# A fused two-block model on one core: second input's squares in pairs, S5 lag matrices in full, S5 parameter chain in two parts

## The chip, the cores and the metric

One core of one Trainium2 chip. The metric is the device time of one execution in microseconds; the time of a version is the median of its runs.

## What is computed

The reference runs two residual blocks over 1024 tokens of 1024 features, all in float32. Block one: RMS norm, a large input projection, gated linear attention and differential attention side by side, an output projection, then a convolutional gated FFN of width 2816. Block two adds a positional code to the result and applies an "even" mixer and an "odd" mixer. What the change touches is around the even mixer:

```python
xl = x + sincos_2d(n_tok, x.shape[-1])                    # second input
hl = rmsnorm(xl, norm_g[0]) * (1.0 + scale) + shift
# S5: 48 groups of 16 channels, 64 complex states each, both directions
step = exp(log_step); lam_bar = exp(lam * step)
b_bar = ((lam_bar - 1.0) / lam) * b
s = associative_scan(linear_recurrence, (lam_bar, u @ b_bar))
y = s.real @ c_re - s.imag @ c_im      # forward + backward + d * u
```

The kernel evaluates the recurrence in chunks of CT = 8 steps. In a chunk, the output is a product of the chunk's inputs with a block matrix made of per-lag blocks (the lag matrix, 8 x 16 rows for each group), plus a product of the state ahead of the chunk with the matrices called cp.

## The kernel before, in words

The kernel is a chain of stages; each is a block in which the five engines run their own programs and wait on semaphores by count. A projection (`project`, L134) goes strip by strip: SyncE loads a weight strip of 128 x 1024, ScalarE rounds it to a high part, GpSimd makes the low part (L233), TensorE multiplies high by high, high by low and low by high in 128 x 512 tiles (L263), and VectorE or ScalarE evacuates PSUM. Strips 0 and 1 go together. Strip i + 2 waits for its low part and for the evacuation of strip i (in the same PSUM half). The low part of strip i is made on GpSimd in the order of its program.

**Output projection of block one** ("mix", 8 strips). Beside it, `S5Parameters` (L797) computes exp(lam * step), its powers and factors on VectorE in some 80 small dependent operations: `steps` (18) and `angles` (23) ahead of the first evacuation, `first_power` and `raise_powers` behind strip 1's, `factors` behind strip 2's. Every operation waits for the one before it (`then`, L863). `steps` first waits for three loads, issued behind the 4 MB load of x. ScalarE takes two sines behind the high part of strip 2. GpSimd copies the powers (`place_powers`, behind the low part of strip 3, waiting for `raised`) and computes b_bar (`place_inputs`, behind the low part of strip 4), always ahead of the next low part.

**FFN** (`gated_ffn`, L2274). 22 rounds of gate, down and val strips. Beside it, `StepMatrices` builds the S5 matrices for 3 groups in each of 16 rounds: GpSimd forms products, TensorE turns them and forms lag blocks (L2176), VectorE takes these out of PSUM (`take_taps`, L2181) into a tile of 16 partitions, and SyncE stores cp (L2103), then bt (L2108) and the lag tile in one DMA (L2110). `take_taps` waits until the lag tile of the round before is stored, and the next gate strip on TensorE waits for `taken`.

**Entry into block two** (`IntoBlockTwo`, L2533, at the end of the FFN). VectorE scales the eight rows of x; GpSimd adds the code to rows 0 to 3, VectorE to rows 4 to 7 (L2550). For the next RMS norm ScalarE squares each row into one of two buffers (L675) and TensorE adds up each row over the partitions, 8 matmuls with a column of ones on 8 tiles of 128 x 128 (L680). A square waits for the count two rows back. Mean, root and inverse come in the next block (the input projection "u" of the even mixer), in which ScalarE first rounds the context (L2674), GpSimd makes its low part (L2678), and TensorE waits for that ahead of `spread` (L603), which copies the inverse to all partitions.

**Scan and outputs** (`scan_and_outputs`, L2695). VectorE runs the scan over chunks, 159 steps of four small operations. TensorE meanwhile forms the updates, the strips for the z and Fourier parts, and the Fourier transform. Behind the scan come the outputs, 8 batches of 6 groups, over two buffers: TensorE makes, group by group, the lag product (L2919) and two state products (L2921, L2922); VectorE (L3042) and ScalarE (L2989) gather the states, two copies each; ScalarE applies gelu (L2979) and stores. SyncE loads a batch's cp (one DMA) and its lag matrix in eight DMAs, one for each row block of 16 partitions (L2818), once the batch two back is done. So one batch is in work while the next is loaded only if its buffers are free.

```python
def load(b, s, turn, first):
    if not first:
        sp.wait_ge(done, b - 1)
    sp.dma_start(cp[s], ...)
    for j in range(CT):
        a = (CT - 1 - j) * SH
        sp.dma_start(taps[s][j * SH:(j + 1) * SH, :, :], g.dram["taps"][:, bass.ds(b * GB, GB), a:a + P])
```

## Time and profile before

| what | value |
| --- | --- |
| median of 3 runs | 2517.22 us (2515.45 to 2518.70) |
| profiled execution: its time | 2514.42 us |
| profiled execution: span from first to last instruction | 2512.7 us |
| TensorE matmul busy | 2284.7 us (91%) |
| VectorE busy | 1441.7 us (57%) |
| GpSimd, ScalarE busy | 746.1 us (30%), 701.4 us (28%) |
| mean granted TensorE clock | 0.945 |

The page's row of 40 slices shows TensorE at nine tenths or more nearly everywhere in the FFN. The lower digits after the FFN (slice 24, clock digit 6) and around slices 29 and 30 (clock digits 7 and 8) are the entry into block two and the S5 outputs; the dip at slices 9 to 11 is the output projection of block one. In a timeline row the number in brackets is the engine's idle time ahead of the row and what ended it. Where a wait has several conditions the row names the one that came last by the profile; if that was long done, it was another, often a DMA. "x2" merges two instructions, and the start-to-start distance of such rows is the pace.

### The profile page before, as it was taken

The numbers are of one execution on the slowest core, as the hardware profiler recorded it, in microseconds if no ns is written. First come the engines' busy times: TensorE is split into PE (matmuls) and PEld (weight loads), VectorE is DVE, ScalarE is ACT, GpSimd is POOL, SyncE is SP. The second block draws the span as 40 slices with busy tenths as digits, with TensorE's granted clock in tenths as the row PEclk, the third lists the DMA queues.
The fourth block names the chain that finished last, engine by engine and source line by source line (L and its number), as shares of the span: only waits on it lengthen the run. The fifth ranks groups of instructions, "written<-read, shape, count | busy, mean of one in ns | idle before, by whom it ended". The sixth has DMA issues, their size and how long they took to land. (4 is left out here: it accounts for less than half of the span.)

```text
span 2512.7 us, 29091 instructions
## 1 busy us (share of the span) xinstructions
PE 2284.7 (91%) x11596; PEld 1867.8 (74%) x11596; DVE 1441.7 (57%) x2138; ACT 701.4 (28%) x862; POOL 746.1 (30%) x439
## 2 busy tenths in 40 slices
PE   5999987997889999999999989889965898999986
PEld 3887875676667888888888878778845686878875
DVE  4665435894648887677765663329881424731223
ACT  4104412675122222222222223224124322111121
POOL 0212220112517656655662221110000541221240
PEclk8999988999989999999999996899978998999998
DMA  6596421333113333333332111252236322111111
GB/s 244 209 304 183 125 93 52 109 111 134 43 42 97 111 104 105 116 113 113 113 119 73 51 42 67 76 160 83 96 98 197 146 114 70 51 42 51 42 51 67
DMA packets 108303, 264.98 MB, mean 105 GB/s; under 512 B 9415, under 2 KB 52839, under 8 KB 105065
## 3 DMA queue, kind: packets, MB, share of 16 engines
q1 hardware_dynamic: 105172, 258.04, 31.1%
q10 hardware_dynamic: 3000, 5.15, 0.6%
q8 instruction: 89, 1.46, 0.2%
q14 instruction: 42, 0.34, 0.0%
HBM read 222.79 MB, written 57.13 MB: 111 GB/s over the span
## 5 line engine op out<-in xcount | busy, mean ns | idle before, releaser
L2342 POOL TENSOR_TENSOR w_lo<-w_staged,w_hi 128x1024 fp32r<-128x1024 f32 x66 | 162.5, 2462 | 371.6 <-ACT w_hi L2437 371.5
L233 POOL TENSOR_TENSOR w_lo<-w_staged,w_hi 128x1024 fp32r<-128x1024 f32 (+1 forms) x34 | 83.2, 2449 | 254.8 <-ACT w_hi L200 254.7
L1263 PE MATMUL ps_in<-h_hi,w_hi 128*128 128x512 f32 x400 | 126.6, 398 | 9.4 <-DVE h_lo L648 9.1
L1255 POOL TENSOR_TENSOR w_lo<-w_staged,w_hi 128x1024 fp32r<-128x1024 f32 x23 | 58.1, 2527 | 229.1 <-ACT w_hi L1242 229.1
L366 POOL TENSOR_TENSOR w_lo<-w_staged,w_hi 128x1024 fp32r<-128x1024 f32 x24 | 58.0, 2418 | 228.4 <-ACT w_hi L349 228.4
L374 PE MATMUL ps_odd<-o_hi,w_hi 128*128 128x512 f32 x384 | 121.0, 397 | 4.2 <-DVE o_lo L648 4.2
L1263 PE MATMUL ps_in<-h_lo,w_hi 128*128 128x512 f32 x400 | 124.4, 392 | 0.0
L1263 PE MATMUL ps_in<-h_hi,w_lo 128*128 128x512 f32 x400 | 124.0, 391 | 0.0
L2437 ACT CAST w_hi<-w_staged 128x1024 fp32r<-128x1024 f32 x66 | 69.0, 1045 | 188.4 <-PE ps_dn L2378 188.4
L2248 DVE SCALAR_TENSOR_TENSOR ada_acc<-x_ctx,cond,ada_acc 128x512 f32<-128x512 f32 x112 | 119.8, 1100 | 2.0
L374 PE MATMUL ps_odd<-o_lo,w_hi 128*128 128x512 f32 x384 | 118.8, 391 | 0.0
L374 PE MATMUL ps_odd<-o_hi,w_lo 128*128 128x512 f32 x384 | 118.7, 390 | 0.0
L2362 PE MATMUL ps_up<-f_hi,w_hi 128*128 128x512 f32 x352 | 109.9, 394 | 4.6 <-DVE f_lo L648 4.0
L2362 PE MATMUL ps_next<-f_hi,w_hi 128*128 128x512 f32 x352 | 112.1, 400 | 0.0
L2362 PE MATMUL ps_up<-f_hi,w_lo 128*128 128x512 f32 x352 | 109.3, 392 | 0.0
L2362 PE MATMUL ps_up<-f_lo,w_hi 128*128 128x512 f32 x352 | 109.2, 392 | 0.0
L2362 PE MATMUL ps_next<-f_lo,w_hi 128*128 128x512 f32 x352 | 108.6, 390 | 0.0
L2362 PE MATMUL ps_next<-f_hi,w_lo 128*128 128x512 f32 x352 | 108.5, 389 | 0.0
L2487 DVE SCALAR_TENSOR_TENSOR x<-ps_n,mod,x 128x1024 f32<-128x1024 f32 x66 | 84.5, 1280 | 36.8 <-PE ps_n L2378 34.5
L200 ACT CAST w_hi<-w_staged 128x1024 fp32r<-128x1024 f32 (+1 forms) x34 | 34.8, 1024 | 246.4 <-PE ps_u L263 60.7
L1263 PEld LDWEIGHTS ps_in<-h_hi,w_hi 128*128 128x128 f32 x400 | 73.8, 189 | 27.0 <-issue 12.2
L2001 DVE CUSTOM_DVE_ANT_0 att_s<-ps_s,att_bias 128x1024 f32<-128x1024 f32 x64 | 75.8, 1223 | 23.7 <-PE ps_s L1920 14.6
(473 smaller groups left out, 5648.5 us busy)
## 6 DMA issues: line engine op xcount, KB each, us to landing
w_staged<-in_w_ff SPq DMA_DIRECT2D x66, 512.0 KB, 3.6
x_ctx<-in_w_ada SPq DMA_DIRECT2D x48, 512.0 KB, 5.1
x_in<-in_w_ada SPq DMA_DIRECT2D x16, 1024.0 KB, 8.0
scratch_bias<-scratch_line SPq DMA_DIRECT2D x32, 512.0 KB, 7.5
att_bias<-scratch_bias SPq DMA_DIRECT2D x32, 512.0 KB, 3.2
w_staged<-in_w_in SPq DMA_DIRECT2D x17, 512.0 KB, 4.6
ada_w<-in_w_ada SPq DMA_DIRECT2D x8, 1024.0 KB, 19.4
scratch_cp<-ff_shared SPq DMA_DIRECT2D x16, 384.0 KB, 5.8
```

Of the source, the lines that this page charges most:

```text
L200: nc.scalar.copy(st.hi[i % 2][:, 0:widths[i]], st.staged[i % 2][:, 0:widths[i]]).then_inc(st.hi_ready, 1)
L233: nc.gpsimd.tensor_tensor(st.lo[i % 2][:, 0:widths[i]], st.staged[i % 2][:, 0:widths[i]], st.hi[i % 2][:, 0:widths[i]].bitcast(F32), ALU.s ...
L366: nc.gpsimd.tensor_tensor(st.lo[i % 2][:, :], st.staged[i % 2][:, :], st.hi[i % 2][:, :].bitcast(F32), ALU.subtract).then_inc(st.split, 1)
L374: last = nc.tensor.matmul(ps[i % 2][:, a:a + BANK], w[i % 2][:, k * P:(k + 1) * P], r[:, k, a:a + BANK], start=(k == 0 and part == 0), sto ...
L1255: nc.gpsimd.tensor_tensor(st.lo[i % 2][:, :], st.staged[i % 2][:, :], st.hi[i % 2][:, :].bitcast(F32), ALU.subtract).then_inc(st.split, 1)
L1263: last = nc.tensor.matmul(ps[i % 2][:, a:a + BANK], u[i % 2][:, k * P:(k + 1) * P], r[:, k, a:a + BANK], start=(k == 0 and part == 0), sto ...
L2001: nc.vector.tensor_tensor_reduce(e[n % 2][:, i, :], ps_s[:, i, :], bias[n % 2][:, :], 1.0, -3.0e38, ALU.add, ALU.max, top[:, n, i:i + 1]). ...
L2248: v.scalar_tensor_tensor(acc, here, by, acc, ALU.mult, ALU.add).then_inc(self.weighted, 1)
L2342: nc.gpsimd.tensor_tensor(st.lo[i % 2][:, :], st.staged[i % 2][:, :], st.hi[i % 2][:, :].bitcast(F32), ALU.subtract).then_inc(st.split, 1)
L2362: last = nc.tensor.matmul(ps_up[which][:, a:a + BANK], w[i % 2][:, k * P:(k + 1) * P], r[:, k, a:a + BANK], start=(k == 0 and part == 0), ...
L2437: nc.scalar.copy(st.hi[i % 2][:, :], st.staged[i % 2][:, :]).then_inc(st.hi_ready, 1)
L2487: nc.vector.scalar_tensor_tensor(x[:, k, :], ps_dn[k % len(ps_dn)][:, :], gate_f[:, k:k + 1], x[:, k, :], ALU.mult, ALU.add).then_inc(adde ...
```

## The change

Three edits, independent of each other in place.

First, the parameter chain. The load of lam is issued first, with its own semaphore, and `steps` runs on VectorE ahead of the wait for x; `angles` runs behind strip 0's evacuation; the sines go behind the high part of strip 3; `place_inputs` is split in halves, behind the low parts of strips 4 and 5.

Second, the squares. All eight squares have buffers of their own. GpSimd adds two pairs of them (1+0, 2+3), VectorE the others, down to two tiles, and TensorE adds up two tiles over the partitions rather than eight. Mean, root and inverse move into the FFN's block. The wait for the context's low part comes behind `spread`.

Third, the lag matrices. In the FFN each round's lag tile is stored in eight DMAs (three, three and two, over three units of SyncE's program) as the full block matrix, and `take_taps` waits for all eight of the round before. In the outputs a batch is loaded in two DMAs, there are three buffers for it (the third in rows of 1 KB), TensorE makes the lag products of a batch ahead of its state products and those of batches 0 and 1 ahead of the scan's end, VectorE gathers three quarters of the states and ScalarE one, and the Fourier folds come behind the gathers of batches 2 and 3.

```diff
@@ project
             def begin():
+                if beside is not None:
+                    beside.first(sp)
                 for b in before:
                     b.sync(sp)
...
+            if beside is not None:
+                beside.vector(dve, -1)
             for b in before:
                 b.vector(dve)
-            if beside is not None:
-                beside.vector(dve, -1)
@@ S5Parameters
+    def first(self, sp):
+        sp.dma_start(self.lam, self.g.dram["s5_lam"]).then_inc(self.lam_loaded, 16)
...
     def scalar(self, act, i):
-        if i == 2:
+        if i == 3:
             self.sines(act)
     def vector(self, dve, i):
         if i == -1:
             self.steps(dve)
+        if i == 0:
             self.angles(dve)
...
-        if i == 4:
-            self.place_inputs(pool)
+        if i in (4, 5):
+            self.place_inputs(pool, i - 4)
@@ StepMatrices, gated_ffn
-        sp.dma_start(self.g.dram["taps"][:, b * MB:(b + 1) * MB, :], ...).then_inc(self.taps_stored, 16)
+        self.store_lags(sp, b, range(0, 3))
+    def store_lags(self, sp, b, lags):
+        groups = slice((b % 2) * MB, (b % 2 + 1) * MB)
+        for j in lags:
+            sp.dma_start(self.g.dram["toeplitz"][b // 2, j * SH:(j + 1) * SH, groups, :],
+                         self.taps[:, :, CT - 1 - j:2 * CT - 1 - j, :].rearrange(...)).then_inc(self.taps_stored, 16)
...
-            dve.wait_ge(self.taps_stored, 16 * b)
+            dve.wait_ge(self.taps_stored, 16 * CT * b)
...
+                if i >= 9 and i % 3 == 0 and (i - 9) // 3 < mats.N:
+                    mats.store_lags(sp, (i - 9) // 3, range(3, 6))
+                if i >= 10 and i % 3 == 1 and (i - 10) // 3 < mats.N:
+                    mats.store_lags(sp, (i - 10) // 3, range(6, CT))
@@ IntoBlockTwo
+        v, sq = self.nc.vector, self.sq
+        dve.wait_ge(self.squared, 6)
+        v.tensor_tensor(sq[4], sq[4], sq[5], ALU.add).then_inc(self.dve_added, 1)
+        dve.wait_ge(self.pool_added, 2)
+        v.tensor_tensor(sq[1], sq[1], sq[2], ALU.add).then_inc(self.dve_added, 1)
+        dve.wait_ge(self.squared, 8)
+        v.tensor_tensor(sq[6], sq[6], sq[7], ALU.add).then_inc(self.dve_added, 1)
+        dve.wait_ge(self.dve_added, 3)
+        v.tensor_tensor(sq[4], sq[4], sq[6], ALU.add).then_inc(self.dve_added, 1)
+        self.second.mean(dve)
+        self.second.inverse(dve)
...
+        for a, b in ((1, 0), (2, 3)):
+            pool.wait_ge(self.squared, b + 1)
+            pool.wait_ge(self.squared, a + 1)
+            self.nc.gpsimd.tensor_tensor(self.sq[a], self.sq[a], self.sq[b], ALU.add).then_inc(self.pool_added, 1)
...
-        for k in range(KD):
-            self.second.count(pe, k)
+        for half, (ready, sq) in enumerate(((2, self.sq[1]), (4, self.sq[4]))):
+            pe.wait_ge(self.dve_added, ready)
+            for j in range(second.tiles):
+                last = self.nc.tensor.matmul(second.ps[:, j:j + 1], sq[:, j * P:(j + 1) * P], self.g.ones[:, 0:1], ...)
@@ scan_and_outputs
+            load(0)
+            load(1)
+            for s in range(2):
+                sp.wait_ge(z_stored[s], 16 * (KD // 2))
+            sp.wait_ge(by_pe, FNET_IN)
+            load(2)
+            for b in range(ROOMS, N):
+                if b == 5:
+                    for i in range(S):
+                        sp.wait_ge(folded, 3 * (i + 1))
+                        sp.dma_start(g.dram["yf"][i], yf[i]).then_inc(y_stored, 16)
+                sp.wait_ge(done, b - ROOMS + 1)
+                load(b)
...
+            for b in range(2):
+                tap_products(b)
+            for b in range(N):
+                if b >= 2:
+                    tap_products(b)
+                state_products(b)
```

In `tap_products(b)` TensorE waits for the batch's two loads and, from batch 2 on, for the gelu of batch b - 2; in `state_products(b)` for both gathers.

## Rows read from the trace of the kernel before

**Rows 1.** Timeline of VectorE, output projection: start us, us, engine, line, operation, idle before.
```profile
627.84 2.02 DVE L873 TENSOR_SCALAR s_lam<-s_lam 128x48 f32<-128x48 f32 x1 [22.61 <-DMA s_par<-in_s_c]
...
641.54 1.28 DVE L3180 SCALAR_TENSOR_TENSOR x<-ps_mix,mod,x 128x1024 f32<-128x1024 f32 x1
...
654.28 0.36 DVE L927 TENSOR_TENSOR s_pw<-s_pa,s_pb 128x192 f32<-128x192 f32 x1
...
715.73 1.28 DVE L3180 SCALAR_TENSOR_TENSOR x<-ps_mix,mod,x 128x1024 f32<-128x1024 f32 x1 [7.24 <-PE ps_mix L263]
```

**Rows 2.** Timeline of TensorE, same stage; each row is a pair of matmuls.
```profile
642.97 1.19 PE L263 MATMUL ps_mix<-mix_hi,w_hi 128*128 128x512 f32 x2 [5.55 <-DVE x L3180]
...
647.22 0.62 PE L263 MATMUL ps_mix<-mix_hi,w_lo 128*128 128x512 f32 x2
...
666.29 0.61 PE L263 MATMUL ps_mix<-mix_hi,w_lo 128*128 128x512 f32 x2
...
681.23 1.22 PE L263 MATMUL ps_mix<-mix_hi,w_hi 128*128 128x512 f32 x2 [2.79 <-POOL w_lo L233]
```

**Rows 3.** Timeline of GpSimd, same stage.
```profile
611.00 18.80 POOL L731 TENSOR_TENSOR mix_lo<-mixed,mix_hi 128x1024 fp32r<-128x1024 f32 x8 [36.34 <-ACT mix_hi L725]
...
654.71 2.04 POOL L965 COPY s_par<-s_pw 64x432 f32<-64x432 f32 x1 [6.52 <-DVE s_pw L927]
...
664.79 2.42 POOL L233 TENSOR_TENSOR w_lo<-w_staged,w_hi 128x1024 fp32r<-128x1024 f32 x1
...
678.82 5.66 POOL L233 TENSOR_TENSOR w_lo<-w_staged,w_hi 128x1024 fp32r<-128x1024 f32 x2
```

**Rows 4.** Timeline of TensorE, entry into the second block.
```profile
1567.30 3.55 PE L680 MATMUL ps_next<-ones,ff_val 128*128 128x1 f32 x16
...
1577.67 3.78 PE L603 MATMUL ps_next<-consts,rms_cols_n 128*128 128x128 f32 x16 [6.82 <-POOL e_lo L2678]
...
1585.42 1.41 PE L263 MATMUL ps_u<-e_hi,w_hi 128*128 128x512 f32 x3 [3.97 <-DVE e_lo L648]
```

**Rows 5.** Timeline of VectorE, same entry.
```profile
1548.52 4.62 DVE L2550 TENSOR_TENSOR x<-x,consts 128x1024 f32<-128x1024 f32 x4
```

**Rows 6.** Timeline of GpSimd, same entry.
```profile
1540.34 7.48 POOL L2550 TENSOR_TENSOR x<-x,consts 128x1024 f32<-128x1024 f32 x4 [2.12 <-DVE x L2563]
```

**Rows 7.** Timeline of ScalarE, same entry.
```profile
1571.14 1.90 ACT L2674 CAST e_hi<-x_ctx 128x2048 fp32r<-128x2048 f32 x1 [5.97 <-PEq L2302]
```

**Rows 8.** Timeline of TensorE, S5 outputs.
```profile
1877.97 0.77 PE L2919 MATMUL ps_strips<-x,over_lo 128*128 128x128 f32 x2 [16.40 <-ACT over_hi L2989]
...
1882.95 0.39 PE L2919 MATMUL ps_strips<-x,over_lo 128*128 128x128 f32 x2
...
1888.08 0.39 PE L2922 MATMUL ps_strips<-over_hi,over_lo 128*128 128x128 f32 x2
...
1893.55 0.79 PE L2919 MATMUL ps_strips<-x,over_lo 128*128 x2 [5.08 <-ACT over_hi L2989]
```

**Rows 9.** Timeline of ScalarE, S5 outputs.
```profile
1874.99 5.81 ACT L2989 COPY over_hi<-s_hist 64x768 f32<-64x768 f32 x4 [12.37 <-DVE s_hist L3030]
...
1935.70 0.81 ACT L2979 ACTIVATE over_hi<-ps_strips 128x768 f32<-128x768 f32 x1 [3.12 <-PE ps_strips L2922]
```

**Rows 10.** Timeline of VectorE, S5 outputs.
```profile
1874.99 3.04 DVE L3042 COPY over_hi<-s_hist 64x768 f32<-64x768 f32 x4
```

**Rows 11.** DMA view, 1884 to 1900 us: GB/s in 40 slices of 0.4 us.
```profile
GB/s 0 0 0 0 0 100 92 177 108 246 369 399 399 438 408 357 314 286 233 292 369 292 284 315 338 338 372 307 305 205 145 133 60 81 53 21 21 12 0 0
```

**Rows 12.** Timeline of SyncE, FFN.
```profile
1006.73 0.61 SPq L2103 DMA_DIRECT2D scratch_cp<-ff_shared  x1
```

**Rows 13.** Timeline of VectorE, FFN.
```profile
1011.34 0.49 DVE L2189 COPY s_taps<-ps_up 16x336 f32<-16x336 f32 x1 [3.84 <-PE ps_up L2176]
```

**Rows 14.** Timeline of TensorE, FFN.
```profile
1014.08 0.61 PE L2362 MATMUL ps_up<-f_hi,w_hi 128*128 128x512 f32 x2
```

**Rows 15.** All DMAs of line L2103, from issue to landing.
```profile
DMA to landing us min/median/max: 4.7/5.8/6.7
```

More of the change, by code:

```diff
@@ L2987, in batch @@
                     act.wait_ge(done, b - 1)
-                for c in range(2):
-                    last = nc.scalar.copy(states[s][lower, c, :, :], of(lower, NCTX, b, c))
-                last.then_inc(gathered[0], 1)
+                nc.scalar.copy(states[s][lower, 0, :, :], of(lower, NCTX, b, 0)).then_inc(gathered[0], 1)
                 if not (first and s == 0):
@@ L3036, in _, with gather @@
                     low_part(split_behind[m])
[L3038 to L3039 removed]
+            def gather(b):
+                s = b % 2
+                if b >= 2:
                     dve.wait_ge(done, b - 1)
+                nc.vector.tensor_copy(states[s][lower, 1, :, :], of(lower, NCTX, b, 1))
                 for c in range(2):
```

146 lines of the change are left out of this document (79 added, 67 removed).

## The prediction

> **What bounds the kernel now.** The page comes first: TensorE is busy for 91% of the span, so time can come only from the places where it waits or runs at a low granted clock. Its row of slices shows three such places that the diff touches. The timelines of TensorE there, then of the engine each wait names, give the limits.
>
> In the output projection TensorE waits 5.55 us for strip 0's evacuation at 642.97, with VectorE in `angles` until 641.54, and 2.79 us at 681.23 for a low part that GpSimd makes late [rows 1 to 3]. After each wait the matmuls run at the lower of the clock's two levels (1.2 of 2.4 GHz) for some microseconds.
>
> In the entry into block two TensorE counts squares at the low clock until 1570.85, and then waits for the context's low part; the input projection starts only at 1585.42 [rows 4]. In the outputs the scan ends at T = 1874.99 [rows 9], and two batches of products are followed by a wait of 5.08 us [rows 8]. ScalarE is named for that wait, but its copies had been done for microseconds, and the DMA view shows transfers up to the end of the wait [rows 11]: the loads end it.
>
> The FFN between is bound by TensorE without a gap, so there the change can only add.
>
> **The parameter chain.** `steps` has 18 operations; its first, at 627.84, took 2.02 us beside GpSimd's last low part of the mix, and ended as that ended (611.00 + 18.80 = 629.80) [rows 1, 3]. The load of lam, now first, should land near 612.5, so `steps` runs beside the eight low parts of 2.35 us. The row shows one operation held for the rest of a GpSimd instruction; whether each is held, it can't show. If each is, one gets in after each low part: 7 by 629.8, and 11 more at about 0.23 us end at 632 to 633.5. Strip 0 is done at about 633.4 and is evacuated at 634.7 rather than 642.8.
> The Trainium skill, SBUF — State Buffer, section "Who interferes with whom", says that a VectorE operation in a two-port mode or with two SBUF inputs and a reading GpSimd operation exclude each other for a whole instruction, whichever came first. By that rule `steps` fills the time up to strip 0 and pushes the low parts by 0.2 us each; without it `steps` would end at 618. The sum changes by 0.4 us at most.
>
> So the wait of 5.55 us goes: strips 2 and 3 start at once. The pace is (666.29 - 647.22) / 42 pairs = 0.454 us a pair, 10.9 us a strip of 24 pairs; the ramp after a wait costs 4.25 - 5 x 0.454 = 2.0 us [rows 2]. Strip 3 ends at 659.2.
>
> What is late next is strip 4's low part, queued on GpSimd behind `place_powers`, which waits for `raised`. Before: powers raised at 654.64 [rows 1], copied 654.71 to 664.79, low part until 667.21 [rows 3]. After: `angles` starts at 634.7 and is held up twice by low parts (2.4 us each): 4.8 + 23 x 0.23 + about 0.7 for the memsets = 645.5. Then a copy (0.7), strip 1's evacuation (1.2) and the powers, 6.9 without neighbours: 654.3. It is thus raised as before, and strip 4 starts at about 667.1. TensorE waits 7.9 us there and pays one ramp. The gain is not the 5.55 us; the wait moves.
>
> The gain lies behind. Strip 5's low part now waits for half of `place_inputs` only; it came at 678.82 + 2.41 = 681.2, and comes near 675.5, ahead of strip 4's end. The stage ends at 667.1 + 2.0 + 4 x 10.9 = 712.7 rather than at 715.7 (evacuation of the last strip, [rows 1]). Taken: **2.9 us**. Bounds: 0, if the chain is held once more for 3 us; 6, if operations slip in between GpSimd's and powers are raised 3 us earlier. SyncE's one extra small issue ahead of x costs at most 0.6 us of x's landing, which has 10 us to spare.
>
> **The squares.** A count row of 16 instructions takes 3.42 us at the low clock; eight of them with the tail end at 1567.30 + 3.55 = 1570.85 [rows 4]. After: GpSimd's codes end at 1547.82 [rows 6]; its two pair adds (2.35 us each, by the low parts of [rows 3]) and VectorE's four codes (1.16 us, [rows 5]) exclude each other: add until 1550.2, code until 1551.4, add until 1553.7, three codes until 1557.2. Last square 1558.4 (1 us on ScalarE, half of 1.90 in [rows 7]). VectorE's four adds end at 1558.4, 1559.5, 1560.7, 1562.0. TensorE's first half runs 1559.6 to 1563.1, the second to 1566.6. Mean, root and inverse, three small dependent operations: 0.8 us. Block end 1567.4, next block 0.3 us later as before (1570.85 to 1571.14, [rows 4, 7]): 1567.7.
> There `spread` starts at once; before it waited until 1577.67 for the context. From its start to the first product it was 1585.42 - 1577.67 = 7.75 us [rows 4], through VectorE and ScalarE, and stays so: 1575.5. The context's low part (1571.14 + 1.90 + 4.5, before) is now at 1574.3, hidden by that. **9.9 us**. Bounds: 13 if codes and adds don't exclude each other; 8 if they interleave badly.
>
> **The outputs.** Pace of a row of two instructions: 0.42 us at the low clock (12 rows from 1877.97 to 1882.95), 0.223 at the high one (23 from 1882.95 to 1888.08); a batch has 18 rows, 6 of the lag products and 12 of the states [rows 8]. The two lag products that are moved ahead lie in TensorE's idle time ahead of T. A gather on VectorE is three copies of 0.76 us (3.04 / 4, [rows 10]), ScalarE has one of 1.45 (5.81 / 4, [rows 9]) and no longer sets the start. State products of batch 0 from T + 2.4 to T + 7.4 (low clock), batch 1 to T + 10.1; then six batches of 4.0 us, if all comes in time: T + 34.1. The gather of batch b follows batch b - 2 by 2.5 us on VectorE and 3.2 on ScalarE (gelu, store, copy), less than the 4.0 + 1.3 there are.
>
> Whether loads come in time: batch 3's leaves at T + 7.4, its buffer's batch 0 being done. From there 5 loads of 1.18 MB, 1.05 MB of the Fourier output (stored ahead of batch 5's load) and about 5 outputs of 0.39 MB, 8.9 MB in all, must move. The DMA view shows 399 to 438 GB/s in the slices of cp rows (3 KB) and 233 to 372 in those of 512-byte lag rows [rows 11]. All is in 3 KB rows now, but for one buffer in three in 1 KB rows. At 400 it takes 22 us, at 300 it takes 30: with 1.8 us from issue to flow, the last load lands at T + 31.4 to T + 39, and the last batch ends 4.0 later. I take T + 38, nearer the fast rows, with one stall at batch 5. Before, it was 1935.6 = T + 60.6 [rows 9]. **22.6 us**; bounds 17.6 and 26.5 (TensorE's own pace). The tail (gelu, store, reload) is the same.
> The Trainium skill, SBUF — State Buffer, section "A bandwidth-pool intuition that's wrong", gives about 358 GB/s between HBM and a core. The rows exceed it in several slices; by the page's figure the drain would be an estimated 25 us and the batch end T + 38. The measurement decides.
>
> **What the FFN pays.** Of each round's eight lag stores the last two are issued behind cp's of the next round, at 1006.73 + 0.66 and later [rows 12]. cp's stores land after 5.8 us (4.7 to 6.7) [rows 15], and stores behind it somewhat later, taken as 0.2: about 1012.9. `take_taps` now waits for them on VectorE: at 1011.34 it would start 1.6 us later [rows 13], end at 1014.3 (1.3 us for its four operations), and TensorE's next gate strip wants it at 1014.08 [rows 14]. Queued behind it on VectorE are the ada sums and val's taps, which are wanted later. The distance from cp's issue to `take_taps` is 4.6 us in this round; over rounds 1 to 15 it lies between 3.6 and 7.0, mostly near 5.4, where nothing is late. Taken: **1 us** in all; bounds 0 and 5. SyncE's 112 added issues of 0.43 us lie in its waits. GpSimd and TensorE have no new wait.
>
> **Sum.** 2.9 + 9.9 + 22.6 - 1.0 = 34.4 us. Against the profiled execution's 2514.4: 2480.0. That execution is 2.8 us under the median of the runs, of which the three spread over 3.3. Against the median: 2482.8. I give **2482**.
>
> **Rivals.**
> (A) The drain is held by TensorE alone, loads never late, and the chain at its good end: 26.5 + 5 + 10 = 41.5, **2475**. For it speak the 438 GB/s slices, against it yf's stores ahead of batch 5's load.
> (B) The clock stays low in the outputs. Short waits in each batch keep TensorE from the high level: 7.5 us a batch, last at T + 59, gain 2 there: **2503**. For it: after the wait at 1893.55 the rows start low again. Against it: with the same shapes it rose within 5 us of steady work [rows 8].
> (C) Edits that don't do what they say: the lock eats half of the squares' gain and the chain's part is nil, the drain at its slow end: 5 + 0 + 17.6 - 2 = 21, **2496**.
> (D) Slower: the lag stores. If the last of them land at +10 us rather than +6, `take_taps` is late in all 15 rounds and TensorE waits ahead of each gate strip. It decides from 35.4 / 15 = 2.4 us a round; at 4 us with a ramp of 1.8 it costs 87 us: **2569**. Against it: cp's slowest landing is 6.7 us. The Trainium skill, DMA: Bandwidth & Descriptors, section "Anatomy of one DMA — SWDGE (gpsimd) path", puts about 2 us of fixed cost on each DMA, mostly the write's receipt; an estimate from it, were the eight stores serial, would be 16 us a round. The rows show DMAs of one queue overlapping.
>
> **How the numbers follow.** Forecast 0.62, A 0.13, B 0.08, C 0.13, D 0.04. Bounds of the forecast's own terms together: gains of 20.7 to 45, 2472 to 2496. The range takes in A and C: 2471 to 2499. About 0.2% (5 us) is what a measurement of this kernel tells from no change; faster by more 0.94 (the forecast and A to C, less the 2 in 100 in which B and C fall together), within it 0.02, slower 0.04.
>
> **What would show it.** In the profile after: a wait of about 8 us ahead of strip 4 of the output projection and none ahead of strips 2 and 5; u's first product 7.8 us behind `spread`, which starts with the block; state products 2.4 us behind the scan's end, and the last one some 38 us behind it, with no wait over 4 us between; TensorE without gaps in the FFN. The prediction is wrong if waits in the FFN exceed 5 us in all, if the clock in the outputs stays at the low level, or if loads come later than 1.5 us behind each other's demand.

## The result, and the profile after

The changed kernel takes 2488.82 us (median of 4, 2487.07 to 2490.87) against 2517.96 us for the kernel before on the same chip (4 runs, 2515.45 to 2518.80): ratio 0.9888 [0.9876, 0.9900], 29.1 us less. The profiled execution took 2490.87 us, the slowest of its four, with a span of 2489.0 us.

The page of the changed kernel: span, busy time and share by engine, and the rows of slices for TensorE and its clock.
```profile
span 2489.0 us, 28760 instructions
...
PE 2265.9 (91%) x11500; PEld 1846.4 (74%) x11500; DVE 1473.2 (59%) x2150; ACT 690.5 (28%) x854; POOL 750.6 (30%) x441
...
PE   5999987997889999999999996789976898999986
...
PEclk8999999898989999999999997799987998999998
```
TensorE is busy 18.8 us less than before (2284.7), at the same share of 91%, and no clock digit differs by more than one (at the entry, slice 24, it is 7 for 6). So the page alone doesn't tell where 29 us went; the stages do. I cut each trace at eight instructions that both kernels have. The lengths in us:

| stretch, from the mark before | before | before, again | after | after, again |
| --- | --- | --- | --- | --- |
| to GpSimd's low parts of the mix | 611.0 | 612.0 | 615.1 | 615.2 |
| output projection, to the last evacuation of ps_mix | 104.7 | 102.9 | 99.7 | 99.6 |
| FFN, to its last low part (ff_lo) | 790.6 | 790.1 | 792.7 | 794.3 |
| first norm's counts, to the first spread | 28.9 | 31.9 | 32.0 | 31.9 |
| entry, to the second spread | 42.5 | 42.5 | 31.8 | 31.9 |
| to the first product of u | 7.8 | 7.8 | 7.8 | 7.8 |
| u, updates and scan, to its end T | 289.6 | 290.8 | 290.6 | 289.5 |
| S5 outputs, to the first product of glu | 73.5 | 74.7 | 54.2 | 54.0 |
| the rest | 564.2 | 564.3 | 565.2 | 565.1 |

The columns called "again" are the last two experiments. Four stretches differ between the kernels beyond their own scatter, the four that the prediction priced. Two others look as if they did in the first pair of profiles (4.1 us at the start, 3.1 us in the first norm's counts); the experiments come back to them.

**Output projection.** VectorE in the changed kernel (start, us, engine, line, operation; in brackets the idle time ahead and what ended it), to be read against [rows 1].
```profile
617.51 2.31 DVE L885 TENSOR_SCALAR s_work<-s_lam 128x48 f32<-128x48 f32 x1
...
622.21 4.67 DVE L888 SCALAR_TENSOR_TENSOR s_lam<-s_work,s_lam 128x48 f32<-128x48 f32 x2
...
636.12 0.21 DVE L902 TENSOR_TENSOR s_work<-s_lam 128x48 f32<-128x48 f32 x1
637.59 1.28 DVE L3248 SCALAR_TENSOR_TENSOR x<-ps_mix,mod,x 128x1024 f32<-128x1024 f32 x1 [1.26 <-PE ps_mix L265]
```
GpSimd and TensorE, same stage, against [rows 3] and [rows 2].
```profile
615.07 18.80 POOL L737 TENSOR_TENSOR mix_lo<-mixed,mix_hi 128x1024 fp32r<-128x1024 f32 x8 [37.51 <-ACT mix_hi L731]
...
657.20 2.04 POOL L976 COPY s_par<-s_pw 64x432 f32<-64x432 f32 x1 [11.20 <-DVE s_pw L938]
...
667.09 2.37 POOL L235 TENSOR_TENSOR w_lo<-w_staged,w_hi 128x1024 fp32r<-128x1024 f32 x1
```
```profile
669.51 1.22 PE L265 MATMUL ps_mix<-mix_hi,w_hi 128*128 128x512 f32 x2 [6.23 <-POOL w_lo L235]
```
`steps` runs beside the eight low parts. The rows at 617.51 and 622.21 take 2.3 us an instruction (two in 4.67), where the row at 636.12, with GpSimd idle, takes 0.21: one gets in for each low part of 2.35 us. The Trainium skill, SBUF — State Buffer, section "Who interferes with whom", says that a VectorE operation with two SBUF inputs, or in a two-port mode, and a reading GpSimd one exclude each other for a whole instruction. The trace agrees for VectorE, 2.3 us against 0.21. For GpSimd it doesn't show it: the low parts took 18.80 us as before and were not pushed by 0.2 us each. Strip 0 is evacuated 22.5 us behind the start of the low parts (before 30.5), TensorE's waits of 5.55 and 2.79 us are gone, and one of 6.23 us stands at strip 4, on the split of its weights behind `place_powers`.

**Entry.** VectorE, GpSimd and TensorE of the changed kernel, against [rows 4 to 6].
```profile
1552.64 8.26 DVE L2576 TENSOR_TENSOR x<-x,consts 128x1024 f32<-128x1024 f32 x4
...
1570.24 0.17 DVE L582 TENSOR_SCALAR rms_cols_n<-ps_next 128x8 f32<-128x8 f32 x1 [4.68 <-PE ps_next L2627]
```
```profile
1551.89 2.35 POOL L2613 TENSOR_TENSOR ff_val<-ff_val,ff_gate 128x1024 f32<-128x1024 f32 x1
1554.20 3.34 POOL L2613 TENSOR_TENSOR ff_shared<-ff_shared,ada_acc 128x1024 f32<-128x1024 f32 x1
1573.15 4.52 POOL L2725 TENSOR_TENSOR e_lo<-x_ctx,e_hi 128x2048 fp32r<-128x2048 f32 x1 [15.62 <-ACT e_hi L2721]
```
```profile
1563.22 3.57 PE L2627 MATMUL ps_next<-ones,ff_val 128*128 128x1 f32 x16 [20.16 <-DVE ff_val L2598]
...
1571.21 3.75 PE L605 MATMUL ps_next<-consts,rms_cols_n 128*128 128x128 f32 x16 [1.00 <-PEq L2321]
1578.99 1.41 PE L265 MATMUL ps_u<-e_hi,w_hi 128*128 128x512 f32 x3 [4.04 <-DVE e_lo L650]
```
Two rows of counts in place of eight; `spread` starts with the next block at 1571.21, 0.3 us behind the count's mean and root, and nothing waits for the context's low part. VectorE's four codes took 8.26 us (4.62 in [rows 5]) beside GpSimd's two additions. From 1551.89 to the codes' end at 1560.90 it is 9.0 us. GpSimd's second addition took 3.34 us rather than 2.35, about one code of 1.16 us more, and 2.35 + 3.34 + the three codes that are left are 9.2: the two engines take turns.

**S5 outputs.** TensorE and SyncE of the changed kernel, against [rows 8]; SPq rows are issues of transfers. T is 1869.62.
```profile
1856.11 2.94 PE L2977 MATMUL ps_strips<-x,over_lo 128*128 128x128 f32 x24
1872.15 8.05 PE L2986 MATMUL ps_strips<-over_hi,over_lo 128*128 128x128 f32 x48 [13.10 <-DVE over_hi L3113]
1880.04 1.50 PE L2977 MATMUL ps_strips<-x,over_hi 128*128 128x128 f32 x12
...
1884.43 1.60 PE L2977 MATMUL ps_strips<-x,over_lo 128*128 128x128 f32 x12 [0.21 <-DMA over_lo<-scratch_toeplitz]
...
1889.74 1.60 PE L2977 MATMUL ps_strips<-x,over_lo 128*128 128x128 f32 x12 [1.02 <-DMA over_lo<-scratch_toeplitz]
...
1897.14 2.37 PE L2977 MATMUL ps_strips<-x,over_hi 128*128 128x128 f32 x12 [3.12 <-DMA over_hi<-scratch_toeplitz]
1899.30 3.75 PE L2986 MATMUL ps_strips<-over_hi,over_lo 128*128 128x128 f32 x24
1902.89 1.50 PE L2977 MATMUL ps_strips<-x,over_lo 128*128 128x128 f32 x12
...
1908.25 2.84 PE L2986 MATMUL ps_strips<-over_hi,over_lo 128*128 128x128 f32 x24
```
```profile
1880.24 0.52 SPq L2870 DMA_DIRECT2D over_lo<-scratch_cp  x1
...
1881.95 4.14 SPq L2885 DMA_DIRECT2D scratch_yf<-over_hi  x2
1886.13 0.52 SPq L2870 DMA_DIRECT2D over_lo<-scratch_cp  x1
```
The lag products of batches 0 and 1 lie ahead of T; the states' products start 2.5 us behind it. Batches wait 0.21, 1.02 and 3.12 us for their lag load, and batch 5 (1897.14) then runs mostly at the lower clock level: 2.37 + 3.75 us against 1.50 + 2.84 for the others. The granted clock is 0.65 over the first of these rows and 0.50 from 1899.30 to 1901.00. The last batch ends at 1911.1 = T + 41.5. The load of batch 5 is issued at 1886.13, behind two stores of yf that held SyncE from 1881.95. The DMA view, GB/s in 40 slices of 0.5 us from 1880 us:
```profile
GB/s 289 295 326 404 326 406 406 436 393 438 381 393 393 412 424 424 418 442 389 440 401 418 369 383 387 385 383 424 414 381 408 424 412 422 406 424 412 418 412 418
DMA packets 3491, 7.97 MB, mean 398 GB/s; under 512 B 223, under 2 KB 1375, under 8 KB 3488
```

**FFN.** The longest sum of waits of VectorE in it (us in total, times, longest):
```profile
DVE s_taps L2208 <- DMA scratch_toeplitz<-s_taps: 57.3, 13, 5.8
...
DVE s_taps L2208 <- PE ps_up L2195: 5.6, 2, 4.2
```
In the kernel before, the same operation waited too, for TensorE's products:
```profile
DVE s_taps L2189 <- PE ps_up L2176: 47.2, 14, 5.3
```
The same view of TensorE in the changed kernel, its row on the same tile, and in its second profile a row on VectorE's `mod`, which comes behind `take_taps` and for which the kernel before never waits:
```profile
PE ps_up L2385 <- DVE s_taps L2213: 1.9, 4, 0.8
```
```profile
PE ps_up L2385 <- DVE mod L2289: 1.2, 2, 0.9
```
The 128 lag stores, from issue to landing:
```profile
DMA to landing us min/median/max: 2.8/4.5/5.4
```
And, in the round of [rows 13], the last two stores of the round before and `take_taps`:
```profile
1006.24 1.62 SPq L2129 DMA_DIRECT2D scratch_toeplitz<-s_taps  x2
```
```profile
1011.98 0.50 DVE L2208 COPY s_taps<-ps_up 16x336 f32<-16x336 f32 x1 [5.61 <-DMA scratch_toeplitz<-s_taps]
```
In 13 of 15 rounds VectorE waits for the lag stores of the round before. But 57.3 + 5.6 us are only 15.7 more than the 47.2 that it waited anyway: `take_taps` is late by 1.2 us a round on average. VectorE's next waits, for ScalarE's `ff_val`, shrink from 63.5 to 47.6 us and so take up nearly all of it. TensorE waited for the tile in four rounds.

### The profile page after: what moved, and what is told of

The parts are those of the page before. It is cut to its first block and busy times, and to the rows that moved or that the text cites. A ratio compares the mean times of both kernels' runs of the same rounds, so it can differ in the third digit from the quotient of the medians.

```text
span 2489.0 us, 28760 instructions
## 1 busy us (share of the span) xinstructions
PE 2265.9 (91%) x11500; PEld 1846.4 (74%) x11500; DVE 1473.2 (59%) x2150; ACT 690.5 (28%) x854; POOL 750.6 (30%) x441
## 5 line engine op out<-in xcount | busy, mean ns | idle before, releaser
L2013 DVE CUSTOM_DVE_ANT_0 att_s<-ps_s,att_bias 128x1024 f32<-128x1024 f32 x64 | 75.8, 1223 | 24.9 <-PE ps_s L1932 15.3
```

What stands on the lines that cost most here:

```text
L2013: nc.vector.tensor_tensor_reduce(e[n % 2][:, i, :], ps_s[:, i, :], bias[n % 2][:, :], 1.0, -3.0e38, ALU.add, ALU.max, top[:, n, i:i + 1]). ...
```

## Experiments

Each was timed against the kernel before on its own chip. "Stage" is a length from the table above, taken from that kernel's profile. Three kernels have one part of the change each.

**The chain alone.** The kernel before with:
```diff
-        if i == 2:
+        if i == 3:
             self.sines(act)
...
+        if i == 0:
             self.angles(dve)
...
-        if i == 4:
-            self.place_inputs(pool)
+        if i in (4, 5):
+            self.place_inputs(pool, i - 4)
```


> The kernel before with the chain's edit alone (the parameter chain ahead of and behind strip 0, the wide multiplications one strip later and in two halves, the sines one strip later); squares and outputs of the S5 as before. Theory (the three edits don't touch one another, and each is worth what its stage lost between the two traces): the output projection ends about 5 us earlier relative to its start, the whole kernel is 3 to 6 us faster than before, ratio 0.9976 to 0.9988. Rival (the 5 us is chance of one profiled execution, or is given back by the gated FFN, which ends on its own transfers): within 1 us of before, ratio 0.9996 to 1.0004.


Measured: 2511.52 us against 2518.72, ratio 0.9973 [0.9963, 0.9982]; output projection 100.6 us, FFN 790.3. That is 7.2 us by the medians, somewhat more than the 3 to 6 expected, and more than the 3.7 us by which the output projection is shorter than the mean of the kernels without the edit (104.3); the lags' experiment comes back to that. The rival (no gain) is out, and the FFN gives nothing back.

**The squares alone.** The kernel before with:
```diff
-            self.second.square(act, k)
+            self.nc.scalar.activation(self.sq[k], self.x[:, k, :], ACT.Square).then_inc(self.squared, 1)
+        self.second.root(act)
...
-        for k in range(KD):
-            self.second.count(pe, k)
+        for half, (ready, sq) in enumerate(((2, self.sq[1]), (4, self.sq[4]))):
```


> The kernel before with the edit of the squares alone (pairs added ahead of the counts, mean and root worked out behind them, context rows waited for by the last of the entry). Theory: the entry of block two is 10 to 11 us shorter from the first spread to the first product of u, and the kernel 9 to 12 us faster, ratio 0.9952 to 0.9964. Rival (the u stage was due later anyway, since its weights, its stores and the first matrices are what ends it): under 5 us, ratio over 0.998.


Measured: 2504.70 us against 2518.72, ratio 0.9946 [0.9932, 0.9960]; entry 31.9 us (10.6 less, as expected), the outputs 71.6 where they had no edit. By the medians it is 14.0 us, above the 9 to 12 expected. The gain of the entry reaches the end.

**The lags alone.** The kernel before with:
```diff
+        for j in lags:
+            sp.dma_start(self.g.dram["toeplitz"][b // 2, j * SH:(j + 1) * SH, groups, :],
...
-    LOADS = 16 * (CT + 1)
+    LOADS = 32
```


> The kernel before with the edit of the lag matrices and the S5's outputs alone (lag matrices stored whole in the FFN's rounds, loaded in one transfer a batch, three load buffers, lag products ahead of the state products, folds beside the batches). Theory: 19 us in the output stage less 2 us of waits in the FFN, so 15 to 19 us faster, ratio 0.9925 to 0.9940, and the sum of the three parts is the whole 29 us within 2 us. Rival (the parts help one another, for instance the shorter entry lets transfers for the outputs start earlier): the three sum to under 25 us.


Measured: 2503.59 us, ratio 0.9939 [0.9925, 0.9953]; outputs 54.5 us, FFN 793.4, output projection 104.8. Its own time is in the range; that the three parts sum to the whole within 2 us was a miss. By the ratios the three parts give 6.8 + 13.6 + 15.4 = 35.8 us, against 28.2 for the whole; all three share one baseline, whose error counts three times, and the half-widths of their intervals add up to 9.4 us, more than the difference of 7.6. The stages say more: each part changes its own stages by what the whole change does (the outputs of the squares' kernel, 71.6 us against 73.3 to 74.7 in the others without the edit, are the one stray). And 6 us of the surplus lie where no edit is: the profiles of the chain's and of the squares' kernel, both taken at those kernels' medians, have the first norm's counts at 28.9 us each, and the kernel before, profiled again at its median, has them at 31.9. So no stage shows a gain of one part that another gives back; why those kernels ran at the shorter value stays open.

**All pair additions on VectorE.** The changed kernel with:
```diff
+        for a, b in ((1, 0), (2, 3)):
+            dve.wait_ge(self.squared, max(a, b) + 1)
+            v.tensor_tensor(sq[a], sq[a], sq[b], ALU.add).then_inc(self.pool_added, 1)
         dve.wait_ge(self.squared, 6)
...
-        for a, b in ((1, 0), (2, 3)):
-            pool.wait_ge(self.squared, b + 1)
```


> The changed kernel with all six pair additions of the squares on VectorE and none on GpSimd. VectorE's additions of codes took 8.26 us each beside GpSimd's work there against 4.62 in the kernel before. Theory 1 (the pair additions by GpSimd share the port and stretch VectorE's codes): the codes fall back to 4.6 us, two additions of 1.1 us are added to VectorE's queue, and the first product of u comes 1 to 3 us earlier than 39.6 us behind the first spread. Theory 2 (GpSimd's own additions of codes stretch them; the change only moved their overlap): the codes stay at over 7 us, and the time is within 1 us of the changed kernel's, which is 29 us under before.


Measured: 2488.48 us against 2518.72, ratio 0.9881 [0.9865, 0.9896]. VectorE in that kernel:
```profile
1552.38 4.62 DVE L2576 TENSOR_TENSOR x<-x,consts 128x1024 f32<-128x1024 f32 x4
```
The codes are back at 4.62 us, so GpSimd's pair additions stretched them (theory 1), and the entry is 1.2 us shorter (30.6). In the whole time that can't be told from the changed kernel. (The expectation's "8.26 us each" is the time of all four codes.)

**The Fourier stores last.** The changed kernel with:
```diff
             for b in range(ROOMS, N):
-                if b == 5:
-                    for i in range(S):
-                        sp.wait_ge(folded, 3 * (i + 1))
-                        sp.dma_start(g.dram["yf"][i], yf[i]).then_inc(y_stored, 16)
                 sp.wait_ge(done, b - ROOMS + 1)
                 load(b)
+            for i in range(S):
+                sp.wait_ge(folded, 3 * (i + 1))
+                sp.dma_start(g.dram["yf"][i], yf[i]).then_inc(y_stored, 16)
```


> The changed kernel with the two stores of the Fourier half (yf) behind all the loads of the S5's outputs, rather than ahead of batch 5's. In the changed kernel the lag products of batch 5 waited 3.1 us for their load and TensorE ran at half clock behind it. Theory (SyncE issues load 5 late because of the two stores and their waits, 1881.95 to 1886.13): the wait for batch 5 falls under 0.5 us, the stage from the scan's end to the first product of glu is 3 to 5 us shorter than 54.2 us, and the kernel 3 to 5 us faster. Rival (loads move at the memory's rate and the two stores, 0.8 MB, only change places with them, landing in the last batches or ahead of what follows the outputs): within 1.5 us of the changed kernel.


Measured: 2484.35 us against 2518.26, ratio 0.9868 [0.9852, 0.9885]; outputs 49.9 us, 4.3 less. (The two stores are 512 KB each, 1.05 MB and not the 0.8 that the expectation says.) TensorE there (T is 1865.91):
```profile
1894.22 1.50 PE L2976 MATMUL ps_strips<-x,over_lo 128*128 128x128 f32 x12
...
1898.85 1.60 PE L2976 MATMUL ps_strips<-x,over_lo 128*128 128x128 f32 x12 [0.44 <-DMA over_lo<-scratch_toeplitz]
```
Batch 5 (1894.22) doesn't wait and the clock stays at the higher level; batch 7 waits 0.44 us. The last batch ends at T + 37.2. The theory held: with the bytes unchanged, the order of the stores alone takes batch 5's wait away.

**Small loads.** The changed kernel with:
```diff
+                part = P if b < 3 else 16
-                sp.dma_start(cp_room[s], g.dram["cp"][b].rearrange("p c i n -> p (c i n)").rearrange("p (r t) -> p r t", t=cp_room[s].shape[-1])
+                sp.dma_start(cp_room[s][0:part], g.dram["cp"][b, 0:part].rearrange("p c i n -> p (c i n)").rearrange("p (r t) -> p r t", t=cp_room[s].shape[-1])
```


> The changed kernel in which the C matrices of batches 3 to 7 are loaded for 16 of 128 partitions only (7/8 of five transfers of 786 KB are left out, so that the outputs of those batches are computed from what lies in the buffers). Theory (the transfers' bytes at some 400 GB/s, against TensorE's 5 us a batch, set the pace of the outputs): the waits for batches 3 to 5 are gone and the last batch is done at 35 us or less behind the scan's end rather than 41.5, so 5 to 8 us faster. Rival (TensorE and the issue of the transfers set the pace, not the bytes): 2 us or less faster, with the wait for batch 5 still there.


Measured: 2483.56 us against 2518.26, ratio 0.9861 [0.9844, 0.9879]; outputs 48.1 us, 6.1 less, last batch at T + 35.4, just above the 35 expected, with 0.22 us waited at batch 5. With the yf stores where they are, taking bytes away cures the stall as well; moving the stores had cured 4.3 of the 6.1. Both fit one cause: loads and stores ran at 398 GB/s without a pause for 20 us, and batch 5's load stood behind 1 MB of yf.

**Two load buffers.** The changed kernel with:
```diff
-    cp_room = [free_lo[:, 2 + 2 * s:4 + 2 * s, 0:GB * P] for s in range(2)] + [low[:, 0:2 * GB * P // LC, :]]
-    tap_room = [free_lo[:, 6 + s, 0:GB * P].unsqueeze(1) for s in range(2)] + [u_f[:, 0:GB * P // LC, :]]
+    cp_room = [free_lo[:, 2 + 2 * s:4 + 2 * s, 0:GB * P] for s in range(2)]
+    tap_room = [free_lo[:, 6 + s, 0:GB * P].unsqueeze(1) for s in range(2)]
...
-            load(2)
```


> The changed kernel with two load buffers for the S5's outputs rather than three, all else alike (whole lag matrices, two transfers a batch, lag products ahead). The prediction put the gain of the outputs down to three things at once. Theory (the third buffer is needed, since a load of 1.2 MB takes 2.7 to 3 us at the memory's rate plus its issue and landing of 2 us, and with two it starts only when the batch two before is done): TensorE waits at every batch from 2 on, the last batch is done some 50 us behind the scan's end and the stage is 8 to 12 us longer than 54.2. Rival (one transfer in place of eight is nearly the whole gain): under 3 us longer.


Measured: 2502.79 us against 2518.75, ratio 0.9934 [0.9921, 0.9948]; outputs 70.1 us, 15.9 more. TensorE there:
```profile
1880.27 2.93 PE L2976 MATMUL ps_strips<-x,over_lo 128*128 128x128 f32 x12 [4.82 <-DMA over_lo<-scratch_toeplitz]
1882.99 4.41 PE L2985 MATMUL ps_strips<-over_hi,over_lo 128*128 128x128 f32 x24
...
1895.10 1.68 PE L2976 MATMUL ps_strips<-x,over_lo 128*128 128x128 f32 x12 [3.68 <-DMA over_lo<-scratch_toeplitz]
1896.57 4.44 PE L2985 MATMUL ps_strips<-over_hi,over_lo 128*128 128x128 f32 x24
...
1902.10 1.60 PE L2976 MATMUL ps_strips<-x,over_lo 128*128 128x128 f32 x12 [1.09 <-DMA over_lo<-scratch_toeplitz]
```
A miss on the high side: I had expected 8 to 12, and the last batch some 50 us behind the scan's end, where it was 57.5. Nor did every batch wait: batch 3 didn't; batches 2 and 4 to 7 waited 4.82, 3.68, 1.09, 1.29 and 4.40 us, 15.3 in all against 4.4 with three buffers. The wait of 4.82 us was followed by most of a batch at the lower clock (2.93 + 4.41 us for 1.50 + 2.84), the one of 3.68 by a clock that fell in the batch (1.68 + 4.44); behind 1.09 us it stayed high. Without the third buffer 15.9 of the outputs' 19.1 us are gone. The other 3 are what the rest of the edit gives with two buffers (fewer transfers, lag products ahead of the scan's end, the split of the gathers); which of these gives it wasn't tested.

**Powers one strip later.** The changed kernel with:
```diff
-        if i == 3:
+        if i == 4:
             self.place_powers(pool)
-        if i in (4, 5):
-            self.place_inputs(pool, i - 4)
+        if i in (5, 6):
+            self.place_inputs(pool, i - 5)
```


> The changed kernel with the powers' placement on GpSimd one strip later (at strip 4 in place of 3) and the two halves of the inputs at 5 and 6. In the changed kernel GpSimd places the powers ahead of the split of strip 4's weights, and TensorE waits 6.2 us for those, then runs some 2 us slower until its clock is back. Theory (the split of strip 4's weights has only to stand ahead of the placement): the wait at strip 4 is gone and no wait over 1.5 us takes its place, the output projection is 6 to 9 us shorter, the kernel 6 to 9 us faster than the changed one. Rival 1 (the wait only moves to strip 5, since 9.8 us of placement stand ahead of its weights then): within 2 us. Rival 2 (the projection gains, but the first matrices of the S5 steps, which need the powers and the inputs, then start late in the FFN and it gives the gain back): 3 us or less, with the FFN longer.


Measured: 2482.19 us against 2518.26, ratio 0.9858 [0.9842, 0.9875]; output projection 93.8 us, 5.9 less, FFN as in the changed kernel. TensorE and GpSimd there:
```profile
673.60 0.69 PE L265 MATMUL ps_mix<-mix_hi,w_hi 128*128 128x512 f32 x2 [1.73 <-DVE x L3248]
```
```profile
651.33 2.39 POOL L235 TENSOR_TENSOR w_lo<-w_staged,w_hi 128x1024 fp32r<-128x1024 f32 x1 [8.50 <-ACT w_hi L202]
...
657.14 2.05 POOL L976 COPY s_par<-s_pw 64x432 f32<-64x432 f32 x1 [2.54 <-DVE s_pw L938]
```
The split at 651.33 now stands ahead of the placement. The wait at strip 4 is gone. One of 1.7 us stands at strip 5 (673.60), for an evacuation that comes behind VectorE's factors; the expectation had none over 1.5. The stage's 5.9 us are just under the range of the theory, the 6.6 of the medians in it.

**All lag stores of a round at once.** The changed kernel with:
```diff
-        self.store_lags(sp, b, range(0, 3))
+        self.store_lags(sp, b, range(CT))
...
-                if i >= 9 and i % 3 == 0 and (i - 9) // 3 < mats.N:
-                    mats.store_lags(sp, (i - 9) // 3, range(3, 6))
-                if i >= 10 and i % 3 == 1 and (i - 10) // 3 < mats.N:
-                    mats.store_lags(sp, (i - 10) // 3, range(6, CT))
```


> The changed kernel with all eight lag stores of a round issued in one slot (where the first three stand) rather than in three slots. In the changed kernel VectorE waited 57.3 us in all for the lags to be stored before it evacuated the next ones, and TensorE 1.9 us for VectorE, four times; and the first norm's counts behind the FFN ran 3.0 us longer at half clock, which the kernel with the lag edit alone showed too (+3.0) and the kernels with the other edits alone did not (+0.0). Theory 1 (the stores' late issue is what VectorE waits for): TensorE's four waits vanish, the FFN is 1.5 to 2.5 us shorter. Rival (eight stores in one slot hold SyncE 4.5 us, and the weights' loads queued behind them come late): new waits of TensorE for weights, and the FFN is no shorter. For the counts: if their low clock hangs on when the FFN's stalls fall, it changes with these waits, and the counts are back at 28.9 us from the last low part to the spread (3 us more gained); if it hangs on something else of the lag edit (its memory traffic, its buffers), it stays at 31.9.


Measured: 2484.68 us against 2518.26, ratio 0.9870 [0.9851, 0.9890]; FFN 790.3 us, 2.4 less than in the changed kernel and as in the kernel before (theory 1). VectorE's and TensorE's waits for the lag stores are gone from the list, and no wait for weights has come. SyncE's eight issues took 4.3 us in one piece:
```profile
1017.01 4.32 SPq L2129 DMA_DIRECT2D scratch_toeplitz<-s_taps  x8
```
The first norm's counts were back at 28.9 us too, so I took their clock for a consequence of the waits.

**The three together.** The edits of the Fourier stores, the powers and the lag stores above, in one kernel.


> The changed kernel with three edits together: the yf stores behind all loads of the outputs (alone 4.3 us in the output stage), the powers and inputs placed one strip later (alone 5.9 us in the output projection), all eight lag stores of a round in one slot (alone 2.4 us in the FFN and 3.1 us in the first norm's counts behind it). Theory (each works in a stage of its own): 14 to 17 us faster than the changed kernel, 2471 to 2476 us, ratio to before 0.982 to 0.984. Rival (the stages share transfers or clock states, so that one gives back another's gain, as the three parts of the change might have): under 12 us.


Measured: 2475.20 us (5 runs, 2472.49 to 2477.28) against 2518.75, ratio 0.9821 [0.9808, 0.9835]. Stages against the changed kernel: output projection 5.9 less, FFN 3.1, outputs 3.7. That is 12.7 us by the stages and 13.6 by the medians, a little under the 14 to 17 expected (the time and the ratio are in their ranges), since the counts' 3.1 us that I had added for the lag stores stayed away: they took 31.8 us with no wait in the FFN. This is the fastest version run, 43.6 us under the kernel before.

**Each kernel once more.** The kernel before, and the changed one, unchanged.


> The kernel before, unchanged, profiled once more. In ten profiles the stretch from the last low part of the FFN to the first spread took either 28.9 us (before, chain alone, squares alone, lags at once, two rooms) or 31.9 us (after, lags alone, adds by VectorE, yf last, powers late, small loads, all three), by the clock of the first norm's last two rows of counts. With the waits of the FFN taken away it was 28.9 in one kernel and 31.9 in another, so the waits don't decide it. Theory (chance of each execution, whatever the kernel): 28.9 or 31.9, and the part ahead of the output projection scatters by some us too (611.0 in the first profile, 612.0 to 615.5 in the others). Rival (the kernel decides): 28.9 again.

> The changed kernel, unchanged, profiled once more. Theory (the clock of the first norm's counts is chance of each execution): 31.9 or 28.9 us from the last low part of the FFN to the first spread; if either of these two kernels shows the other value than in its first profile, the kernel doesn't decide it. Rival (the kernel decides): 31.9 again. In both cases the output projection (99.7 us), the entry (31.8), and the outputs (54.2) agree with the first profile within 1 us each, since those differences are the change's.


Measured: 2518.80 us against 2519.05, ratio 1.0002 [0.9990, 1.0014], and 2489.70 us, ratio 0.9887 [0.9858, 0.9917]. The stages are in the table: output projection, entry and outputs of the changed kernel agree with its first profile within 0.3 us. The last two rows of the first norm's counts, in the kernel before, once more, and in the two-buffer kernel:
```profile
1529.83 2.87 PE L680 MATMUL ps_up<-ones,ff_gate 128*128 128x1 f32 x16
1532.56 3.55 PE L680 MATMUL ps_up<-ones,ff_val 128*128 128x1 f32 x16
```
```profile
1530.97 1.93 PE L682 MATMUL ps_up<-ones,ff_gate 128*128 128x1 f32 x16
1532.76 1.93 PE L682 MATMUL ps_up<-ones,ff_val 128*128 128x1 f32 x16
```
The kernel before now shows the low level (3.55 us a row, 31.9 in all) and the two-buffer kernel, with all the FFN's waits, the high one (1.93, 28.9). So neither the change nor the waits decide it: the stretch takes one of two values from one execution to the next. (The expectation says ten profiles and lists twelve.) Of the fourteen profiles nine show the low level: eight of the ten of kernels with the lag edit, one of the other four. Whether the edit shifts the odds these can't tell; by those counts it would be worth some 1.7 us ((0.80 - 0.25) x 3.1), and so would count against the lag edit. Nor is the start the change's in any way that the runs show: 611.0 and 612.0 before, 610.4 to 615.5 in the others; what sets it stays open.

## Why the prediction was right, and where it was off

The forecast case came: 2482 against 2488.8, inside the range, faster. None of the rivals came. Of the prediction's own signs of being wrong one did: a load later than 1.5 us behind its demand, batch 5's with 3.12. The total is nearer than its two largest errors together, since chain and squares gave more than forecast. The four terms, each as the mean over the profiles that have the part against those that haven't:

| term | predicted | measured |
| --- | --- | --- |
| chain | 2.9 (0 to 6) | 104.3 - 100.4 = 3.9 |
| squares | 9.9 (8 to 13) | 42.5 - 31.9 = 10.6 |
| outputs | 22.6 (17.6 to 26.5) | 73.3 - 54.2 = 19.1 |
| FFN | -1 (0 to -5) | 790.4 - 793.7 = -3.3 |
| sum | 34.4 | 30.3 |

The kernels with an edit inside a stage are left out of its mean. The difference of 4.1 us is the outputs' 3.5 and the FFN's 2.3, less 1.0 and 0.7 that chain and squares gave more. The other 2.7 of the 6.8 us: the sum was set against 2517.2 and before measured 2518.0 (0.7), 2482.8 was rounded down to 2482 (0.8), and the medians show 29.1 where the stages sum to 30.3 (1.2, within the interval). The prediction's bounds add up to 20.6 and 45.5 rather than 20.7 and 45, on which nothing hangs.

**Chain.** "The gain is not the 5.55 us; the wait moves" held: 6.23 us at strip 4, where 7.9 were forecast, no wait at strips 2 and 5. The powers were raised 42.1 us behind the start of the low parts (657.17) rather than the 43.3 that the prediction's 654.3 means, since strip 0 was evacuated 22.5 us behind it rather than 23.7. The experiment with the powers later confirms that this wait is what is left of the stage.

**Squares.** The working came out nearly instruction by instruction: the counts begin 23.8 us behind the first spread, where 24.4 were forecast; 7.78 us from spread to product, 7.75 forecast. The alternation of codes and additions is shown by the kernel with the additions on VectorE. The lock stretched the codes by 3.6 us, and taking the two additions off GpSimd gives back 1.2: rival C's half of the gain is out.

**Outputs.** The failed step is the sentence "with 1.8 us from issue to flow, the last load lands at T + 31.4 to T + 39, and the last batch ends 4.0 later". It treats the transfers as one lump whose end counts. The rate was right (400 taken, 398 measured over 20 us), and the last load was in time: batches 6 and 7 didn't wait. What counted was batch 5's load in the middle. The pace came to T + 34.7 (2.5 to the first states, 7.9 for two batches, six of 4.02, 0.2 for the last one's end); on it lie 0.21 + 1.02 + 3.12 us of waits and (2.37 - 1.50) + (3.75 - 2.84) = 1.8 us of low clock: 40.8 of the 41.5. "One stall at batch 5" was foreseen, but neither its length nor the clock behind it had a term. A drain has to be checked batch by batch, each against its own load. With the stores of yf moved, the last batch ended at T + 37.2, and with the bytes cut at T + 35.4, near the bound of rival A (T + 34.1).
The Trainium skill, SBUF — State Buffer, section "A bandwidth-pool intuition that's wrong", gives about 358 GB/s between HBM and a core, half of a stack's 716. From 1882.5 us on the slices stand at 369 to 442, reads and stores together, so the trace exceeds the figure.

**FFN.** Mechanism and sign were right, the size was not: 3.3 us rather than 1. For the round of [rows 13] the working holds. `take_taps` starts 6.4 us behind cp's issue (1005.61), where 6.2 were taken; counted from the last evacuation of ps_mix it is 1.7 us later than before, forecast 1.6; and TensorE's gate strip waits 0.28 us. But "mostly near 5.4, where nothing is late" was too good: VectorE was late in 13 rounds, by 15.7 us in all, and its slack hid most of that. The FFN took 2.3 us (first profile) and 3.9 us (second) more than the mean before. TensorE's waits on the tile are 1.9 and 2.1 us of this; its waits for the evacuation of x fell by 0.6 (2.1 to 1.5); and in the second profile the 1.2 us on `mod` are added, so what is queued behind `take_taps` was not always "wanted later". About 1 us in each profile is named by no wait and stays open, though the kernel with all stores at once shows the whole of it gone (790.3). Rival D needed 2.4 us a round and is far off. The 2 us a DMA beside D are, in the Trainium skill, DMA: Bandwidth & Descriptors, section "Anatomy of one DMA — SWDGE (gpsimd) path", those of a DMA that GpSimd issues. The lag stores are SyncE's, and they overlap: with all stores at once, eight were issued in 4.32 us, and one landed after 3.9 us in the median.

**Rival B** came for one batch instead of all: 1.8 us. The two-buffer kernel shows it for three batches of six: 3.0, 1.8 and 1.8 us more than the 4.34 of a batch at the higher level.

## What to carry to other kernels

Where several transfers feed a pipeline, work out each batch's landing against its own demand; a buffer more was worth 15.9 us here (from two to three), and the order of two stores 4.3. When a chain is shortened, look at what stands next in the queue of the engine that releases the bottleneck: the wait of 6.2 us at strip 4 went, and one of 1.7 at strip 5 came, by issuing one operation ahead of another. A sum of waits is no measure of lateness where the engine waited before as well: of 57.3 us here 15.7 were new. Compare stages and not only spans, and profile the unchanged kernel a second time before a difference in code that nobody touched is given a cause.

## What the runs showed that was not expected

- With GpSimd at work on wide additions, a VectorE operation on 48 columns took 2.3 us rather than 0.2, one for each of GpSimd's, and GpSimd was not slowed by it (18.80 us for eight, with or without). Beside VectorE's wide additions one of GpSimd's did take longer, 3.34 us for 2.35.
- The same stretch of single-column counts ran at one of two clock levels from one execution to the next and so took 28.9 or 31.9 us. The unchanged kernel before showed both; so did kernels with the lag edit.
- A wait of 3.12 us in the outputs was followed by 6.1 us of work, mostly at the lower clock, for 4.3 at the higher one, so that stall cost 1.8 us more than it shows; behind a wait of 1.02 us the clock stayed high, and the batch took 0.1 us more.
- The FFN of the changed kernel took 792.7 and 794.3 us in two profiles. Of the 1.6 us between them 1.2 are TensorE's waits in the second for `mod`, a small VectorE operation behind `take_taps`.
